# A decoder step on one core: two plain up chunks, caches rolled beside both layers, a convolution tap on ScalarE

## The reference, cut to what matters

```
h    = rmsnorm(x, g)
gate = h @ w_up[:, :2816];  up = h @ w_up[:, 2816:]
conv = b + t0*gate[t-2] + t1*gate[t-1] + t2*gate[t]      # per channel
x    = x + (silu(conv) * up) @ w_down
```

## Time and profile before

| | us |
|---|---|
| median of 3 runs | 3058.94 (3054.68 to 3059.58) |
| the profiled execution | 3060.31 |
| its span | 3058.4, granted TensorE clock 0.972 |
| busy in the span: PE, DVE, ACT, POOL | 2842.8 (93%), 1863.8 (61%), 1053.0 (34%), 677.6 (22%) |

### The profile page before, as it was taken

How to read it: one execution, slowest core, us unless ns; L and a number is a source line. 1 busy time by engine, 2 the same in 40 slices (tenths; PEclk the granted TensorE clock), 3 DMA queues, 4 the chain that set the end, 5 groups by cost and what they waited for, 6 DMA issues and landing times. The chain is left out here.

```text
span 3058.4 us, 52884 instructions
## 1 busy us (share of the span) xinstructions
PE 2842.8 (93%) x20722; PEld 2604.6 (85%) x20722; DVE 1863.8 (61%) x3319; ACT 1053.0 (34%) x1847; POOL 677.6 (22%) x482
## 2 busy tenths in 40 slices
PE   8999999888899888999989999988897999999998
PEld 7888899778888888999988666655797999999998
DVE  3445444545877777765553444468449888886555
ACT  4444311333322222245543333322223323334544
POOL 3101222004322223200121000034043333340001
PEclk9999999999999999999999999999898999999999
DMA  6121111751377775277742000157311222226776
GB/s 195 54 67 52 33 51 46 290 221 49 105 237 246 236 237 178 97 245 224 226 141 69 15 15 1 53 212 304 112 56 42 70 80 80 69 70 195 223 220 209
DMA packets 280684, 406.79 MB, mean 133 GB/s; under 512 B 21914, under 2 KB 218548, under 8 KB 272884
## 3 DMA queue, kind: packets, MB, share of 16 engines
q1 hardware_dynamic: 272056, 295.32, 30.2%
q0 software_dynamic: 8448, 108.93, 9.9%
HBM read 357.66 MB, written 112.19 MB: 154 GB/s over the span
## 5 line engine op out<-in xcount | busy, mean ns | idle before, releaser
L1098 PE MATMUL psum<-mlp_halves,mlp_operands 128*128 128x352 f32 x4032 | 685.1, 327 | 66.5 <-DVE mlp_combine L1471 39.5
L1098 PEld LDWEIGHTS psum<-mlp_halves,mlp_operands 128*128 128x128 f32 x4032 | 661.4, 192 | 74.0 <-DVE mlp_combine L1471 44.1
L1175 PE MATMUL psum<-mlp_ring 128*128 128x352 f32 x3168 | 517.9, 324 | 7.0 <-issue 4.4
L1175 PEld LDWEIGHTS psum<-mlp_ring 128*128 128x128 f32 x3168 | 511.0, 188 | 9.5 <-issue 7.4
L918 DVE TENSOR_TENSOR mlp_ring<-mlp_ring_whole,mlp_ring 128x864 fp32r<-128x864 f32 x264 | 286.0, 1090 | 207.0 <-ACT mlp_ring L912 205.5
L1866 PE MATMUL psum<-h_ab,w_in_halves 128*128 128x352 f32 x2016 | 340.5, 326 | 3.3 <-PEq L281 2.3
L1866 PEld LDWEIGHTS psum<-h_ab,w_in_halves 128*128 128x128 f32 x2016 | 321.8, 189 | 17.1 <-issue 10.9
L912 ACT CAST mlp_ring<-mlp_ring_whole 128x864 fp32r<-128x864 f32 x264 | 241.1, 915 | 274.1 <-DMA mlp_ring_whole<-products_spill 274.0
L1098 PE MATMUL psum<-mlp_turns,mlp_operands 128*128 128x352 f32 x1512 | 260.9, 321 | 0.0
L1098 PEld LDWEIGHTS psum<-mlp_turns,mlp_operands 128*128 128x128 f32 x1512 | 243.9, 188 | 0.0
L607 PE MATMUL psum<-mlp_halves,project_w 128*128 128x352 f32 x1152 | 188.9, 326 | 8.3 <-DVE project_w L635 8.3
(11 more groups left out here) (369 smaller groups left out, 4224.8 us busy)
## 6 DMA issues: line engine op xcount, KB each, us to landing
mlp_ring_whole<-in_w_down SPq DMA_DIRECT2D x264, 256.0 KB, 2.8
mlp_ring_whole<-products_spill SPq DMA_DIRECT2D x264, 176.0 KB, 3.6
mlp_raw<-in_w_up SPq DMA_DIRECT2D x66, 512.0 KB, 4.1
out_new_a_k_s<-in_cache_a_k POOLq DMA_DIRECT2D x8, 4088.0 KB, 15.1
out_new_a_v_s<-in_cache_a_v POOLq DMA_DIRECT2D x8, 4088.0 KB, 15.2
products_spill<-window SPq DMA_DIRECT2D x44, 528.0 KB, 4.0
w_in_raw<-in_w_in_ab SPq DMA_DIRECT2D x28, 512.0 KB, 4.5
mlp_raw_up<-in_w_up SPq DMA_DIRECT2D x22, 512.0 KB, 3.9
```

The source lines that it names most:

```text
L1098: mm = nc.tensor.matmul(c.bank[bank][:, 0:TILE], operands[:, operand, w, k, :], tokens(x, k), start=begin and k + w + x == 0, stop=end and ...
L1175: mm = nc.tensor.matmul(c.bank[bank_set(at) + o][:, 0:TILE], slot[:, w, o * P:(o + 1) * P], slot[:, x, self.WIDE:], start=k + w + x == 0, ...
```

## The change

- Chunk (0,1) becomes plain as well, in both layers: its gate tiles go to banks 0, 1, 2 and its up tiles to 3, 5, 7 when DVE has multiplied chunk (0,0). Its weights are split whole, in two parts (`split_second`). The first combined chunk is (1,0); its operands and the token sums are made while chunk (0,1) runs.
- POOL begins the token sums when the norm's last tile is inverted, not when the projection is added; the third token sum is formed between the weight sums of chunk (1,0).
- `roll` goes to both layers: keys beside layer 0's up phase, values beside layer 1's. Each round of POOL's loop (two chunks) has one copy, ahead of its first sums.
- The first tap of every convolution is an ACT activation (`first_tap`), put behind ACT's fifth hi part; DVE makes the lo part of SUM_1 meanwhile.

```diff
-    ORDER_FIRST = (SUM_2, SUM_4, SUM_1, SUM_3, GATE_1, GATE_2, UP_1, UP_2)
+    ORDER_FIRST = (GATE_1, GATE_2, UP_1, UP_2, SUM_2, SUM_4, SUM_1, SUM_3)
+    ORDER_LAST_PLAIN = (1, 0, 2)
+    PLAIN_BANKS = ((0, 1, 2), (3, 5, 7))
...
-        return g * 2 + (self.call * (FC - 1) + s - 1)
+        return g * 2 + (self.call * (FC - 2) + s - 2)
...
+                def first():
+                    sp.wait_ge(self.first_split, START + call * 3 + 1)
+                    self.load_gate(sp, 0, 1)
+                    self.wait_up(sp, 0, 1)
+                    self.load_up(sp, 1, 0)
+                    sp.wait_ge(self.first_split, START + call * 3 + 2)
+                    self.load_gate(sp, 1, 0)
+                    sp.wait_ge(self.first_split, START + call * 3 + 3)
+                    self.wait_up(sp, 1, 0)
+                    self.load_up(sp, 1, 1)
+                    keep(0, 0)
+                    wait_gate_used(1, 0, 2)
+                    self.load_gate(sp, 1, 1)
...
+                    for n in range(TILES):
+                        up_tile(1, 0, n)
+                    pe.wait_ge(self.multiplied, START + (chunk(0, 0) + 1) * (TILES + 1))
+                    for n in self.ORDER_LAST_PLAIN:
+                        up_tile(1, 1, n)
...
-                    if second:
-                        multiplied()
                     products(self.BANK_2, self.GATE_2, tokens(1, 0), True, True)
                     products(self.BANK_LAST_GATE, self.GATE_2, tokens(1, 2), False, True)
                     split_of(self.SUM_1)
                     turned_of(2)
+                    if second:
+                        multiplied()
                     products(self.BANK_5, self.SUM_1, turns(self.TURN_1), True, True)
...
+                def first_tap(g, s, first):
+
+                    def tap(w):
+                        return c.taps[:, layer, w, bass.ds(g * 2 + s, 1)].rearrange("p a -> p a")
+
+                    act.wait_ge(self.gate_taken, START + (chunk(g, s) + 1) * TILES)
+                    if not first:
+                        act.wait_ge(self.multiplied, START + (chunk(g, s) - 1) * (TILES + 1))
+                    nc.scalar.activation(conv[s][:, 0:CONV_OUT], window[s][:, 0:CONV_OUT], ACT.Identity, bias=tap(3), scale=tap(0)).then_inc(self.conv_step, 1)
...
+                def first():
+                    self.wait_gate(act, 0, 1)
+                    nc.scalar.copy(operands[:, 4:6, 0].rearrange("p a k n -> p a (k n)"),
+                                   self.raw_gate.rearrange("p (h k) n -> p h (k n)", h=2)).then_inc(self.first_hi, 1)
+                    self.wait_up(act, 0, 1)
+                    nc.scalar.copy(operands[:, 6:8, 0].rearrange("p a k n -> p a (k n)"),
+                                   self.raw_up[1].rearrange("p (h k) n -> p h (k n)", h=2)).then_inc(self.first_hi, 1)
+                    first_tap(0, 0, True)
+                    silu(0, 0)
+                    self.wait_gate(act, 1, 0)
+                    self.wait_up(act, 1, 0)
+                    act.wait_ge(self.up_ready, START + call * 2 * TILES + TILES)
+                    for operand in ORDER_FIRST[0:4]:
+                        make_hi(1, 0, operand)
+                    turn_high(self.TURN_2, self.turns_formed, call * 7 + 4)
+                    turn_high(self.TURN_1, self.turns_formed, call * 7 + 2)
+                    turn_high(self.TURN_4, self.fourth_formed, call + 1)
+                    refill(0, 1, 1, 0, ORDER_FIRST[4:6])
+                    first_tap(0, 1, True)
+                    silu(0, 1)
+                    turn_high(self.TURN_3, self.turns_formed, call * 7 + 7)
+                    refill(0, 1, 1, 0, ORDER_FIRST[6:8])
...
+                def group(g, second, last):
+                    copy_first(g, 0, second)
+                    refill(g, 0, g, 1, ORDER[0:5])
+                    first_tap(g, 0, False)
+                    refill(g, 0, g, 1, ORDER[5:7])
+                    silu(g, 0)
+                    refill(g, 0, g, 1, ORDER[7:8])
+                    copy_first(g, 1, False)
+                    if not last:
+                        refill(g, 1, g + 1, 0, ORDER[0:5])
+                        first_tap(g, 1, False)
+                        refill(g, 1, g + 1, 0, ORDER[5:7])
                     else:
-                        copy_first(g, 0, False)
-                        refill(g, 0, g, 1, ORDER[0:7])
-                        silu(g, 0)
-                        refill(g, 0, g, 1, ORDER[7:8])
-                    copy_first(g, 1, first)
-                    if not last:
-                        refill(g, 1, g + 1, 0, ORDER[0:7])
-                    else:
+                        first_tap(g, 1, False)
...
-                pool.wait_ge(project.added, START + (project.chunks0 + KC - 1) * TILES + 2)
+                pool.wait_ge(norm.inverted, START + (sums.call + 1) * TILES)
...
+                def form_third():
+                    pool.wait_ge(self.turns_split, START + call * 4 + 1)
+                    hi_2, lo_2 = (x.bitcast(F32) for x in halves_of_turn(self.TURN_2))
+                    hi_11, lo_11 = (h[:, x, 0:HALF, tokens_of(0)].bitcast(F32) for x in range(2))
+                    pool.wait_ge(self.up_ready, START + call * 2 * TILES + TILES + 1)
+                    tt(into_3, hi_2, hi_11, ALU.subtract).then_inc(self.turns_formed, 1)
+                    pool.wait_ge(self.turns_formed, START + call * 7 + 5)
+                    tt(into_3, into_3, lo_2, ALU.add).then_inc(self.turns_formed, 1)
+                    pool.wait_ge(self.turns_formed, START + call * 7 + 6)
+                    tt(into_3, into_3, lo_11, ALU.subtract).then_inc(self.turns_formed, 1)
+
+                def first_waits(operand):
+                    if operand in (self.SUM_2, self.SUM_4):
+                        pool.wait_ge(self.gate_ready, START + (call + 1) * 2 * TILES)
+                    else:
+                        if operand == self.SUM_1:
+                            form_third()
+                        pool.wait_ge(self.up_ready, START + (call + 1) * 2 * TILES)
+
+                self.form(pool, 1, 0, first_waits)
...
-                if roll:
-                    with pool.Fori(0, DEC_BATCH) as i:
-                        roll.roll(pool, i, 0)
-                        refill(i + 1, 0, i + 1, 1, lambda: roll.wait_rolled(pool, i, 0))
-                        roll.roll(pool, i, 1)
-                        refill(i + 1, 1, i + 2, 0, lambda: roll.wait_rolled(pool, i, 1))
-                    for g in range(1 + DEC_BATCH, LAST_GROUP):
-                        group(g)
-                else:
-                    with pool.Fori(0, GROUPS - 2) as i:
-                        group(i + 1)
+                group(1)
+                with pool.Fori(0, DEC_BATCH) as i:
+                    roll.roll(pool, i, call)
+                    refill(i + 2, 0, i + 2, 1, lambda: roll.wait_rolled(pool, i, call))
+                    refill(i + 2, 1, i + 3, 0)
...
-                    nc.vector.tensor_scalar(conv[s][:, 0:CONV_OUT], window[s][:, 0:CONV_OUT], tap(0), tap(3),
-                                            ALU.mult, ALU.add).then_inc(self.conv_step, 1)
+                    between()
...
-                    convolve(g, s, False)
-                    refill(self.SUM_1, self.SUM_3, self.UP_1)
+                    convolve(g, s, lambda: refill(self.SUM_1))
+                    refill(self.SUM_3, self.UP_1)
...
+                def split_second():
+                    for x, source in enumerate((self.raw_gate, self.raw_up[1])):
+                        dve.wait_ge(self.first_hi, START + call * 3 + 2 + x)
+                        split_plain(slice(4 + 2 * x, 6 + 2 * x), source.rearrange("p (h k) n -> p h (k n)", h=2))
+
+                def low(*operands):
+                    for operand in operands:
+                        self.make_lo(dve, 1, 0, operand, ORDER_FIRST)
+
+                def first():
+                    banks = [c.bank[b] for b in self.PLAIN_BANKS[1]]
                     old_gates(0, 0, True)
+                    plain_gates(0, split_second)
+                    convolve(0, 0, lambda: None)
+                    scale_conv(0, 0)
+                    multiply(0, 0, banks, lambda n: dve.wait_ge(self.up_ready, START + call * 2 * TILES + n + 1))
+                    low(*ORDER_FIRST[0:4])
                     form_fourth()
                     dve.wait_ge(self.fourth_formed, START + call + 1)
                     turn_low(self.TURN_2, 1)
                     turn_low(self.TURN_1, 2)
                     turn_low(self.TURN_4, 3)
+                    old_gates(0, 1, True)
+                    plain_gates(1, lambda: None)
+                    convolve(0, 1, lambda: low(self.SUM_2, self.SUM_4))
+                    scale_conv(0, 1)
+                    multiply(0, 1, banks, lambda n: dve.wait_ge(self.up_ready, START + (call * 2 + 1) * TILES + max(2, n + 1)))
                     turn_low(self.TURN_3, 4)
```

(32 more changed lines are left out.)

135 lines of the change are left out of this document (39 added, 96 removed).

## The result

The changed kernel takes 3096.26 us (median of 4 runs, 3092.10 to 3099.68) against 3059.26 for the kernel before in the same comparison: ratio 1.0121, interval 1.0101 to 1.0140, so 37 us slower where 49 were forecast. The profiled execution has 3097.35 us, with a span of 3095.8.

The account below looks back on a forecast made before the run. PE was taken as the bound, never idle in layer 1's steady part, with layer 0's rolls costing 60.2 us. 3060.3 + 59.8 (rolls) + 0.6 (tap) - 11 (start) = 3109.7, less 1.4: 3108 us, range 3042 to 3138.

Parts of the forecast that it names:

- A roll per two chunks costs more than one per chunk: Combined chunks, both layers: sixteen pairs at 7.5 us cost 120 us, against 60.2 before: +59.8, bounds +5 and +81.
- 8.1 less 0.7: Rolled pair's extra: 8.8 us less SUM_1's lo part gives 8.1; 0.7 off as the middle of two low-clock costs.
- a single example: Chunk behind the last roll, kernel before: P2 waits 5.61 us and the chunk lasts 29.8 us, 8.8 above 21.0.
- The first tap: Convolution's first tap on ACT: DVE's saved time worth nothing; 0.3 us lost at each layer's last chunk, 0.6 in all.
- the bound: Tap's time on ACT: taken as silu's 1.10 us, bounded by 0.84 (the DVE form) and twice silu.
- The start: Start of each up phase: waits fall from 21.5 to 14 us; gain 5.6 per layer, 11 in all, bounds -39 and +4.
- the two waits: Start of up phase, kernel before: 9.07 us during DVE's token splits and 12.43 us before P2 of chunk (0,1).
- the multiply I named: Start, chunk (1,0): P5 waits about 6 us for the second multiply, two taps, silu and scaling further on.
- Rival 1: Chunk behind a rolled one pays only 4.1 us, POOL's sums fitting between DVE's instructions: 3054 us, chance 0.16.
- Rival 2: Gate load gets past the roll, landing within about 12 us; both layers at 21.0 us a chunk: 2988 us, chance 0.10.
- Rivals 3 and 4: 3: start relieved in full (-39), 3080 us, chance 0.07. 4: DVE stays late between rolls or after start, 3145, chance 0.09.

Follow-up runs that it names:

- the held kernel: Changed kernel with POOL's weight sums, in the chunk behind a roll, waiting for the previous chunk's seventh combining add: 3025.49 us, ratio 0.9899 to the kernel before.
- the kernel with halves: Changed kernel with each roll cut into two halves of rows, one per chunk, still ahead of the gate load: 2972.46 us, ratio 0.9734 to the kernel before.

## Why the prediction was right

Direction and mechanism held, the size was 12 us too high.

- **A roll per two chunks costs more than one per chunk.** Forecast 7.5 us a pair (8.1 less 0.7 is nearer 7.4), 120 in all, +59.8; measured 7.8, 124.7 and +64.5. Landings of 16.1 to 17.2 us, sixteen waits at P2 of about 5.3, and a low clock behind each (24 matmuls in 5.67 us in the changed row, 3.8 at full clock) are as forecast. That a chunk without a roll is dearer because POOL comes early rested on a single example; sixteen waits of that kind show that it is the rule, and the first pair of the held kernel shows the cause. The prediction said that a load ends with its roll, but not why; the packets show it.
- **The first tap.** That the tap itself brings no gain and no loss held. The 0.7 us a pair, 11 us in all, that the sum took off for SUM_1's lo part is not there: with the tap back on DVE the combined chunks take the same 979 us. Without that term a pair would have been forecast at some 8.1 us, against 7.8 measured. The tap takes 1285 ns, more than the 1.10 that I took from silu and inside the bound. The Trainium skill, "ScalarE: Activation LUTs", section "What ACT_TABLE_LOAD costs", with its 93 ns for each per-partition operand, had given an estimate of 1.29; the trace agrees. At the layers' ends PE's wait for DVE (L1192, was L1175) is 1.15 in place of 0.70, together 0.9 us where I had 0.6.
- **The start is the term that was mis-sized**: 11 us forecast, 24.8 measured by the two stretches (12.1 and 12.7); the kernel with the rolls as before gains 24 in all. In layer 0 the kernel before needs those 92.2 us for 408 matmuls (64.9 us at 0.159) and 2 us of the norm: 25.3 lost, of which I had counted the 21.5 of the two waits and not the low clock behind them (granted 0.89 over the stretch, 0.96 after). The changed kernel needs 80.1 us for 420 matmuls (66.8) and the same 2: 11.3 lost, where I had 14 without any low clock. PE waits there 4.25 and 3.42 us, not 7 and 6: the norm ends about 2 us earlier than I worked out, DVE's stretch to the gates is 37.9 us and not 39.3, and P5 was held by SUM_1's lo part and not by the multiply I named.
- **The sum with measured terms**: 3060.3 + 64.5 + 0.9 - 24.8 = 3100.9. The profiled execution has 3097.35; the 3.5 us between lie in stages that the change does not touch, or are not resolved.
- **The rivals.** Rival 1's condition, POOL's sums out of DVE's way, is what the held kernel sets up. It pays 3.6 us a pair over layer 0 and 1.8 in the first pair, where the rival had 4.1; in the changed kernel the condition is not met. Rival 2 asked for landings within 12 us; they are 16 and more, and the kernel with halves shows that at 9.7 it would have come true. The Trainium skill, "DMA: Bandwidth & Descriptors", section "Queues, rings and completion order", states that a DMA engine takes turns between its queues packet by packet. The trace agrees with that, by 48 packets of each queue between 899.0 and 908.8 us. What the prediction drew from it, that a load would be slowed and not held, left out the size of a packet: against 64 KB a turn the load's 512 bytes a turn come to being held. Rivals 3 and 4 did not occur: some 8 us of waits remain at each start, and DVE is back on time after every pair.

## What to carry to other kernels

A long background copy can hold a short load that is issued just behind it almost to its own end. What that costs depends on the time that the engines behind the load have to spare, and on what the wait then sets off: here VectorE and GpSimd in turns, and the low clock. So issue it behind the landing, or cut it until its length fits the spare time, and see that nothing on the path waits for the copy itself. Smaller packets for the copy are another way, which no run here tried. Thinning out a cost that is partly hidden by its own repetition can raise it: here the next roll had been keeping GpSimd out of VectorE's way.

## What the runs showed of the hardware

- A 4088 KB copy within HBM on one queue holds a 512 KB load issued just behind it on another almost to its end (landing 16.1 to 17.2 us instead of 3.7), because the queues pass one packet for one and the copy's packets carry 64 KB, the load's 512 bytes (48 and 48 packets, 3.14 and 0.02 MB, in 9.8 us). The same copy issued after the landing leaves the loads at 3.8.
- VectorE's smallest copies suffer most in proportion beside GpSimd: 128x16 elements take 0.17 us alone and 3.11 beside a token sum of 4.41, and the copy ends at 801.27, the sum at 801.24. The Trainium skill, "SBUF — State Buffer", section "SBUF: two separate sides", describes an exclusive lock in which the loser waits for a whole instruction of the other; the row agrees.
- Behind a wait of 4.64 us at P2 24 matmuls take 5.67 us, and the granted clock of that stretch (884.5 to 890.2) is 0.70, part of it at the lower level of 1.2 GHz; behind one of 1.58 us in the held kernel 23 take 3.94 and it stays at 1.00, the level of 2.4 GHz.
